# Differential attention on one core: attention by query blocks, with each head's last steps issued inside the next head

## What is computed

```python
def block(args):
    qb, bi = args
    ...
    bias = jnp.where(rel[None] >= 0, -slopes[:, None, None] * rel[None].astype(jnp.float32), -jnp.inf)
    s = jnp.einsum('bqhcd,bkhcd->bhcqk', qb, k).astype(jnp.float32) * scale
    p = jax.nn.softmax(s + bias[None, :, None], axis=-1)
    w = p[:, :, 0] - lam * p[:, :, 1]
    return jnp.einsum('bhqk,bkhe->bqhe', w.astype(v.dtype), v)
...
o = rmsnorm(o, subln_g, SUBLN_EPS) * (1.0 - lam_init)
return o.reshape(B, S, V_WIDTH) @ w_o
```

## Time and profile before

| | us |
|---|---|
| median of 3 runs | 1158.46 (1155.45 to 1159.59) |
| the profiled execution, device time | 1158.65 |
| its span, first to last instruction | 1156.8 |
| TensorE busy | 1109.6 (96%) |
| VectorE busy | 613.1 (53%) |
| ScalarE busy | 472.9 (41%) |
| GpSimd busy | 108.4 (9%) |

### The profile page before, as it was taken

The page is one execution under the profiler, slowest core; times in us unless marked ns, Lnnn a source line. Parts: engine busy times, 40 slices in busy tenths (PEclk is TensorE's granted clock), DMA queues, the critical chain, the costliest instruction groups (busy, mean ns, idle before and its releaser), DMA issues.

```text
span 1156.8 us, 13824 instructions
## 1 busy us (share of the span) xinstructions
PE 1109.6 (96%) x4854; PEld 883.9 (76%) x4854; DVE 613.1 (53%) x940; ACT 472.9 (41%) x731; POOL 108.4 (9%) x95
## 2 busy tenths in 40 slices
PE   8999999999999999999999899889999999999995
PEld 4676788888888888888866566668888888888884
DVE  4676965434434434446477877866433433433434
ACT  5475754313313313434246456654422322322342
POOL 0000021000000000021013322322000000000023
PEclk8999999999999999999999999999999999999998
DMA  5222232332322232233221111123223223223322
GB/s 206 73 73 73 73 110 92 99 102 91 97 103 91 92 107 91 92 108 107 76 74 37 54 37 54 37 73 100 101 92 109 92 91 106 94 91 101 98 73 73
DMA packets 30293, 102.42 MB, mean 89 GB/s; under 512 B 3248, under 2 KB 5552, under 8 KB 30128
## 3 DMA queue, kind: packets, MB, share of 16 engines
q1 hardware_dynamic: 29968, 100.74, 26.1%
q10 hardware_dynamic: 288, 1.18, 0.3%
HBM read 99.81 MB, written 2.10 MB: 88 GB/s over the span
## 4 chain that ended last, share of the span: by engine, by line
PE 83%; DVE 10%; ACT 4%; issue 2%; DMA 1%; SPq 0%; DVEq 0%; ACTq 0%
PE ps L1249 73%; PE ps L1380 4%; ACT prob L663 2%; PE ps L1443 1%; DVE prob L1140 1%; DVE w_lo L780 1%; DVE prob L1137 1%; PE ps L1417 1%; PE ps L1308 1%; DVE lru_v L874 1%; DVE inv_lam L1135 1%; ACT w_hi L430 1%; PE ps L1313 1%; DVE lru_v L907 1%; DMA w_raw<-weights 1%
## 5 line engine op out<-in xcount | busy, mean ns | idle before, releaser
L430 ACT ACTIVATE w_hi<-w_raw 128x1024 fp32r<-128x1024 f32 x184 | 193.6, 1052 | 240.9 <-PE ps L1249 205.3
L1249 PE MATMUL ps<-h_hi,w_hi 128*128 128x512 f32 x704 | 287.9, 409 | 2.9 <-DVE w_lo L780 2.9
L1249 PE MATMUL ps<-u_hi,w_hi 128*128 128x512 f32 x696 | 279.9, 402 | 4.2 <-DVE u_lo L918 1.9
L1249 PE MATMUL ps<-h_hi,w_lo 128*128 128x512 f32 x704 | 278.0, 395 | 0.0
L1249 PE MATMUL ps<-h_lo,w_hi 128*128 128x512 f32 x704 | 277.6, 394 | 0.0
L1249 PE MATMUL ps<-u_hi,w_lo 128*128 128x512 f32 x696 | 271.1, 390 | 0.0
L1249 PE MATMUL ps<-u_lo,w_hi 128*128 128x512 f32 x696 | 271.0, 389 | 0.0
L780 DVE TENSOR_TENSOR w_lo<-w_raw,w_hi 128x1024 fp32r<-128x1024 f32 x176 | 216.7, 1231 | 29.6 <-ACT w_hi L430 29.5
L1249 PEld LDWEIGHTS ps<-h_hi,w_hi 128*128 128x128 f32 x704 | 134.4, 191 | 36.8 <-DVE w_lo L780 4.6
L1249 PEld LDWEIGHTS ps<-u_hi,w_hi 128*128 128x128 f32 x696 | 130.7, 188 | 37.8 <-issue 5.9
L1249 PEld LDWEIGHTS ps<-h_lo,w_hi 128*128 128x128 f32 x704 | 134.5, 191 | 31.8 <-issue 4.7
(11 more groups left out here) (163 smaller groups left out, 885.1 us busy)
## 6 DMA issues: line engine op xcount, KB each, us to landing
w_raw<-weights SPq DMA_DIRECT2D x184, 512.0 KB, 3.3
x<-x_t SPq DMA_DIRECT2D x8, 256.0 KB, 7.3
y_t<-att SPq DMA_DIRECT2D x8, 256.0 KB, 2.3
gw<-gate_weights ACTq DMA_DIRECT2D x1, 1024.0 KB, 5.4
lam_in<-lam_vecs ACTq DMA_DIRECT2D x1, 128.0 KB, 2.4
vec<-vectors SPq DMA_DIRECT2D x1, 64.5 KB, 4.1
```

The costliest lines, as they stand in the source:

```text
L430: nc.scalar.activation(w_hi[:, t % RING, :], w_raw[:, t % RAWS, :], ACT.Copy).then_inc(whi_done, 1)
L1249: ins = nc.tensor.matmul(ps[:, bank, :], w[:, slot, ws], o[:, k, :], start=(k == 0 and n == 0), stop=(k == NCH - 1 and n == 2))
```

## The change

- The eight heads are written out; the hardware loops over pairs of heads are gone.
- `scores` takes float32 operands for all four j. The copies and subtractions that made `kq_hi` and `kq_lo` are gone, and `kq` has two buffers.
- `combined` no longer divides: it forms p0 + ratio * p1 with ratio = -lambda * total0 / total1, so a row stays larger by the factor total0. The norm that follows is indifferent to it; its epsilon is multiplied by total0 squared in `variance`. One pass over the row is left of two.
- `attend` is done by query block j, right after `transposed` of it: `prob_t` is the stationary operand, a slice of `value` the moving one, and the result has the query on the partition. GpSimd's `value_h` is gone. 10 float32 matmuls of 128 columns take the place of 4 of 128 to 512 columns.
- The norm's sums run along the free dimension: four 128-wide squares with sums on ScalarE (`squares`), all else on 128x4 numbers (`variance`, `sub_guess_of`, `sub_newton`, on VectorE and ScalarE), four 128-wide scalings (`scaled`), then `back` turns the head with four 128x128 transposes. `attended_hi` and `attended_lo` split it from bank 6 straight into `att_hi` and `att_lo`. `sub_sum` is gone.
- GpSimd has no work in the attention; VectorE makes `w_lo` of all tiles.
- Transposes 2 and 3, all four value products and the norm of head h are issued within head h+1, and the last head has a new interleaving with the output projection.

```diff
-            pool.wait_ge(bank_read, T_QK)
-            head_values(0, None, 0)
-            head_values(1, None, 1)
-            head_split_lo(0, None)
-            with pool.Fori(0, (HEADS - 2) // 2) as i:
-                own.enter(i, 4)
-                for k in range(2):
-                    head_values(2 + k, i, k)
-                    sub_newton(k, i)
-                    head_split_lo(1 + k, i)
-                own.leave((HEADS - 2) // 2)
-            head_split_lo(HEADS - 1, None)
-            sub_newton(HEADS - 2, None)
...
+            def squares(h):
+                act.wait_ge(att_mm, QB * (h + 1))
+                for j in range(QB):
+                    ins = nc.scalar.activation(o_square[:, rows(j)], ps[:, BANK_O, rows(j)], ACT.Square,
+                                               accum_out=o_stats[:, h % 2, 0, j:j + 1])
+                ins.then_inc(att_sq, 1)
+
+            def scaled(h):
+                act.wait_ge(sub_rstd, h + 1)
+                if h:
+                    act.wait_ge(back_mm, h)
+                for j in range(QB):
+                    ins = nc.scalar.activation(o_rows[:, rows(j)], ps[:, BANK_O, rows(j)], ACT.Copy,
+                                               scale=o_stats[:, h % 2, 4, j:j + 1])
+                ins.then_inc(o_scaled, 1)
+
+            def attended_hi(h):
+                act.wait_ge(back_mm, h + 1)
+                nc.scalar.activation(att_hi[:, h, :], ps[:, BANK_T, :], ACT.Copy,
+                                     scale=lam_s[:, 6:7]).then_inc(ohi_done, 1)
...
+            for h in range(HEADS):
+                last = h == HEADS - 1
+                if h:
+                    transposed(h - 1, 2)
+                split_hi(T_QK + 2 * h + 1 + RING if not last else T_QK + 2 * h + RING)
+                exps(h, 0)
+                if h:
+                    transposed(h - 1, 3)
+                exps(h, 1)
+                if h:
+                    squares(h - 1)
                 if last:
+                    split_hi(T_QK + 2 * h + 1 + RING)
+                    sub_guess_of(h - 1)
+                transposed(h, 0)
+                if last:
+                    exps(h, 2)
+                if h:
+                    if not last:
+                        sub_guess_of(h - 1)
+                    scaled(h - 1)
+                transposed(h, 1)
                 if not last:
+                    exps(h, 2)
+                if h < HEADS - 2:
+                    split_hi(T_QK + 2 * h + 2 + RING)
                 if last:
+                    exps(h, 3)
+                if h:
+                    attended_hi(h - 1)
                 if not last:
+                    exps(h, 3)
+            h = HEADS - 1
+            transposed(h, 2)
+            transposed(h, 3)
+            squares(h)
+            sub_guess_of(h)
+            scaled(h)
+            attended_hi(h)
...
+            def combined(h, j):
+
+
                 n = (QB - j) * P
                 s = j % 2
-                dve.wait_ge(exp_done, at(a + 1, i, 2 * QB))
-                own.step(nc.vector.reciprocal(inv[:, s, :], total[:, s, :]))
-                own.wait()
-                own.step(nc.vector.tensor_tensor(inv_lam[:, s:s + 1], inv[:, s, 1:2], neg_lam, ALU.mult))
-                own.wait()
-                own.step(nc.vector.tensor_scalar(prob[:, s, 1, 0:n], prob[:, s, 1, 0:n],
-                                                 inv_lam[:, s:s + 1], None, ALU.mult))
-                own.wait()
-                nc.vector.scalar_tensor_tensor(out=prob[:, s, 0, 0:n], in0=prob[:, s, 0, 0:n],
-                                               scalar=inv[:, s, 0:1], in1=prob[:, s, 1, 0:n],
+                dve.wait_ge(exp_done, QB * h + j + 1)
+                own.step(nc.vector.reciprocal(inv[:, s:s + 1], total[:, h % 2, j, 1:2]))
+                own.wait()
+                own.step(nc.vector.scalar_tensor_tensor(
+                    out=ratio[:, s:s + 1], in0=inv[:, s:s + 1], scalar=neg_lam,
+                    in1=total[:, h % 2, j, 0:1], op0=ALU.mult, op1=ALU.mult))
+                own.wait()
+                nc.vector.scalar_tensor_tensor(out=prob[:, s, 0, 0:n], in0=prob[:, s, 1, 0:n],
+                                               scalar=ratio[:, s:s + 1], in1=prob[:, s, 0, 0:n],
                                                op0=ALU.mult, op1=ALU.add).then_inc(prob_done, 1)
...
+            def variance(h):
+
+
+                first = total[:, h % 2, :, 0:1].rearrange("p q o -> p (q o)")
+                own.step(nc.vector.scalar_tensor_tensor(
+                    out=o_stats[:, h % 2, 3, :], in0=first, scalar=SUBLN_EPS, in1=first, op0=ALU.mult,
+                    op1=ALU.mult))
+                dve.wait_ge(att_sq, h + 1)
+                own.wait()
+                nc.vector.scalar_tensor_tensor(
+                    out=o_stats[:, h % 2, 1, :], in0=o_stats[:, h % 2, 0, :], scalar=1.0 / V_DIM,
+                    in1=o_stats[:, h % 2, 3, :], op0=ALU.mult, op1=ALU.add).then_inc(var_done, 1)
+
+            def attended_lo(h):
+                dve.wait_ge(ohi_done, O_ATT + h + 1)
+                nc.vector.scalar_tensor_tensor(out=att_lo[:, h, :], in0=ps[:, BANK_T, :],
+                                               scalar=sub_gain, in1=att_hi[:, h, :], op0=ALU.mult,
+                                               op1=ALU.subtract).then_inc(olo_done, 1)
...
+            for h in range(HEADS - 2):
+                query(h + 1)
+                split_lo(T_QK + 2 * h + 1 + RING)
+                biased(h, 3)
+                combined(h, 2)
+                key(h + 1)
+                if h:
+                    attended_lo(h - 1)
+                split_lo(T_QK + 2 * h + 2 + RING)
+                halved(h)
+                biased(h + 1, 0)
+                combined(h, 3)
+                biased(h + 1, 1)
+                combined(h + 1, 0)
+                combined(h + 1, 1)
+                variance(h)
+                biased(h + 1, 2)
+                sub_newton(h)
...
+                    pe.wait_ge(bank_read, T_QK + 2 * h + 2)
+                if a >= 2:
+                    pe.wait_ge(scores_read, 2 * (a - 1))
+                for c in range(2):
+                    rows = slice(c * HEAD_DIM, (c + 1) * HEAD_DIM)
+                    ins = nc.tensor.matmul(ps[:, BANK_SCORES + 2 * (j % 2) + c, 0:n],
+                                           kq[rows, h % 2, 1, qb * P:(qb + 1) * P],
+                                           kq[rows, h % 2, 0, 0:n], start=True, stop=True)
                 ins.then_inc(scores_mm, 1)
...
+            def attend(h, j):
+                a = QB * h + j
+                qb = QB - 1 - j
+                pe.wait_ge(trans_read, a + 1)
+                if h and j == 0:
+
+                    pe.wait_ge(o_scaled, h)
+                for kb in range(qb + 1):
+                    ins = nc.tensor.matmul(ps[:, BANK_O, qb * P:(qb + 1) * P],
+                                           prob_t[:, j % 2, kb * P:(kb + 1) * P],
+                                           value[:, kb, h * P:(h + 1) * P], start=(kb == 0),
+                                           stop=(kb == qb))
                 ins.then_inc(att_mm, 1)
 
+            def back(h):
+
+                pe.wait_ge(o_scaled, h + 1)
+                pe.wait_ge(trans_read, min(QB * (h + 1) + 2, QB * HEADS))
+                for qb in range(QB):
+                    qs = slice(qb * P, (qb + 1) * P)
+                    ins = nc.tensor.transpose(ps[:, BANK_T, qs], o_rows[:, qs], ident[:, :])
+                ins.then_inc(back_mm, 1)
...
+            for h in range(HEADS - 1):
+                kq_part(h + 1, 0)
+                scores(h, 0)
+                if h:
+                    transposes(h - 1, 2)
+                    attend(h - 1, 0)
+                scores(h, 1)
+                if h:
+                    attend(h - 1, 1)
+                kq_part(h + 1, 1)
+                scores(h, 2)
+                if h:
+                    transposes(h - 1, 3)
+                kq_part(h + 1, 2)
+                if h:
+                    attend(h - 1, 2)
+                    attend(h - 1, 3)
+                kq_part(h + 1, 3)
+                transposes(h, 0)
+                kq_part(h + 1, 4)
+                transposes(h, 1)
+                kq_part(h + 1, 5)
+                scores(h, 3)
+                kq_part(h + 1, 6)
+                if h:
+                    back(h - 1)
+                kq_part(h + 1, 7)
...
+            h = HEADS - 1
+            attend(h - 1, 0)
+            output_part(T_O, (0, 1))
+            transposes(h - 1, 2)
+            attend(h - 1, 1)
+            scores(h, 0)
+            transposes(h - 1, 3)
+            scores(h, 1)
+            output_part(T_O, (2, 3))
+            attend(h - 1, 2)
+            output_part(T_O, (4, 5))
+            attend(h - 1, 3)
+            output_part(T_O + 1, (0, 1))
+            scores(h, 2)
+            transposes(h, 0)
```

(58 more changed lines are left out.)

365 lines of the change are left out of this document (81 added, 284 removed).

## The result

| | us |
|---|---|
| before, median of 4 | 1156.95 (1155.19 to 1159.59) |
| changed kernel, median of 4 | 1129.99 (1128.45 to 1131.19) |
| ratio | 0.9764, 95% interval 0.9737 to 0.9792 |
| the profiled execution of the changed kernel | 1128.45, span 1126.7 |
| predicted | 1132.5, range 1129.0 to 1144.0 |

The kernel became 27 us faster where 26.0 were forecast. First the table of waits of TensorE in the changed kernel, from the last tiles of the shared key and value projection to behind the output projection; it answers to the earlier trace rows.

The account below looks back on a forecast made before the run. TensorE was taken to set the time while waiting for probabilities, as GpSimd blocks VectorE. Waits 20.1 and 5.4 plus clock 4.8, less 3.6 extra work and 0.7 new waits, gave 26.0 us: 1132.5 us, range 1129 to 1144.

Parts of the forecast that it names:

- The bound: Attention: TensorE sets the time but waits for prob; GpSimd blocks VectorE's third combined, an excess of 3.1 us.
- Waits, 20.1 + 5.4 us: TensorE in the attention: waits of transposes for prob go, 20.1 us; other waits go, 5.4; 0.4 for w_lo stays.
- Clock, 4.8 us: Heads 1 to 6: three falls of TensorE's clock behind the waits go, 1.59 us each, 4.8 us.
- TensorE's extra work, +0.45 per head: Scores +0.33, 64-row entry and exit +0.42, sub_sum -0.91, back +0.47, more pieces +0.1; taken as 3.6 us in 8 heads.
- The rival of 1150 us: Value product: weight loads of the float32 passes show, 0.11 each, 2.2 us per head, 17.6 in all; chance 0.07.
- What is late next: Head of 18.6 us: VectorE 14.2 and ScalarE 11.9 busy fit; all new waits charged 0.7 us.
- The margin of the norm's round trip: From value product to back: round trip some 5.5 us against 6.9 us of TensorE work between, margin 1.4 us.
- The sum: Whole kernel: 20.1 + 4.8 + 5.4 - 3.6 - 0.7 = 26.0 us gained, median 1132.5 us.
- New short waits: Attention cycle: small margins pass delays on, one us in each head, 1140.5 us; chance 0.15 together with VectorE staying slow.
- Dearer float32: Scores or value product: 64-row float32 pairs do not overlap (1143.5 us) or weight loads show (1150); chance 0.13.
- VectorE still slow with a small loss (1140.5): VectorE's queue: 3.1 us stay though GpSimd is idle, key late by at most 1 us per head; chance 0.15 with new waits.
- Slower by the norm: Norm's round trip makes TensorE wait in every head, 4.3 us per head at 5.7 excess, 1167 us; chance 0.04.

Follow-up runs that it names:

- e4: Kernel before, with GpSimd's w_lo of each attention head made by VectorE ahead of the fourth combined: 1143.4 us against 1157.51, ratio 0.9877.
- e5: Kernel before, with only the third transposition of every head issued one part (six matmuls) later: 1153.17 us, ratio 0.997.
- e8: Changed kernel with GpSimd kept busy by four scratch subtractions (6.4 us) in each of seven heads, at the old place: 1130.13 us, ratio 0.9778.
- e3: Changed kernel with six unused 512-wide ScalarE copies (4.0 us) ahead of the four scalings of each head's norm: 1150.02 us, ratio 0.9934.
- e10: Kernel before, third transposition one part later and GpSimd's w_lo on VectorE, but behind the fourth combined: 1147.05 us, ratio 0.9907.
- e6: Kernel before, with scores in one float32 product for all four blocks instead of three split products: 1159.22 us, ratio 1.0012.
- e2: Changed kernel with the 64-row scores of heads 0 to 6 issued in two excursions instead of four: 1125.74 us, ratio 0.9721.
- e1: Changed kernel with one w_lo per head (six tiles) given back to GpSimd: 1130.97 us, 0.35 more than the changed kernel.
- e9: Kernel before, with GpSimd's w_lo on VectorE ahead of the fourth combined and the third transposition one part later: 1141.62 us, ratio 0.9867.

## Why the prediction was right, point by point

**The bound.** Right that TensorE waits for probabilities and that VectorE is late because of GpSimd (e4: 2.44 back to 0.48 us). The same instruction has 0.48 us in the changed kernel too, under the 0.6 that was forecast:

```profile
629.40 0.48 DVE L1080 SCALAR_TENSOR_TENSOR prob<-prob,ratio 128x256 f32<-128x256 f32 x1
```

The excess was read too small, 3.1 us. One instruction ahead of the earlier trace rows, in the kernel before, one column takes 1.05 us for 0.16, so it is 4.0:

```profile
635.58 1.05 DVE L1135 TENSOR_TENSOR inv_lam<-inv,lam_s 128x1 f32<-128x1 f32 x1
```

Nor was GpSimd idle all through the quick ones of the earlier trace rows: its `w_lo` started at 748.44, inside the second, which had started first and was not held. Incomplete in the rest: I read the third transposition as the place where a head loses 2.9 us, and took the remainder for TensorE's own work. Moving just that step in the old kernel gave 0.15 us per head (e5). The claim that the new order or an idle GpSimd alone removes this wait holds for the changed kernel as a whole (e8: 2.12 us of `combined`, no wait in the loop). For an idle GpSimd in the old one it is not shown: e4 got rid of GpSimd's `w_lo` alone, and 1.0 us of wait stayed, but the Newton steps still held VectorE for 0.9 and 1.1 us there, more than the wait that was left.

**Waits, 20.1 + 5.4 us.** Right: 0.9 us of idle time is left of 23.6. I had said that the 0.4 for `w_lo` stays; it is 0.7.

**Clock, 4.8 us.** Right: no fall in the attention, and e4 and e5 had none either; a head with a fall has 22.86 us for 21.25, 1.6 as reckoned. The falls come with the long waits: e3, with 2.1 us of wait per head, has two. The one in the last head of e10 shows that several short waits in a row can do it too.

**TensorE's extra work, +0.45 per head.** Too much. A new head is 18.51 us where I had 18.7. Old heads without fall and wait take 18.2 to 18.3 (21.25 less 2.88 in front of the third transposition and 0.16 in front of the next scores; with a fall, 22.86 less 2.99 and 1.59), so the real difference is +0.2 to +0.3. The scores are +0.33 as reckoned (e6), the toll 0.38 for 0.42 (e2), and the rest is my surcharge of 0.1 for more pieces and rounding up. The float32 passes of 128 columns hide their loads of weights:

```profile
622.17 0.83 PE L1382 MATMUL ps<-value,prob_t 128*128 128x128 f32 x6
622.76 0.48 PE L1193 MATMUL ps<-u_hi,w_hi 128*128 128x512 f32 x1
623.08 0.39 PE L1193 MATMUL ps<-u_lo,w_hi 128*128 128x512 f32 x1
```

From the first of six passes to the second matmul behind them, less one 0.23, are 0.68 us: 0.11 each, with six loads, and a quarter of the 0.43 of a 512-column pass is 0.11. (The next matmul is recorded as starting inside the last pass, so the distance to it alone, 0.59 us, is too short; the 0.10 of a transpose in the prediction is 0.11 for the same reason.) The rule of the Trainium skill (TensorE: Matmul & The Clock Gate, The mechanism) that a load overlaps matmuls in flight only across row groups does not hold for these full-array passes. The same section lets a load run ahead if it goes to a background weight buffer, which would fit; no run here tells. The rival of 1150 us, where each load shows, is out. In both kernels a toll does appear where 64-row and 128-row work alternate.

**What is late next.** Nothing in the loop, as forecast. VectorE has 75.47 / 6 = 12.6 us of work in a head where I had 14.2; 0.7 of that is the `w_lo`, 1.2 us where I took 1.9, and 0.9 the slow `inv_lam` that I had missed. ScalarE has 67.16 / 6 = 11.2 for 11.9. The margin of the norm's round trip was put at 1.4 and is 1.7 (e3), but not by my sum: a 128-wide square follows the last one after 0.25 to 0.27 us where I took the 0.40 of an exponential from the earlier trace rows, and the copy of the second transposition, which stands behind the scalings and is what `back` waits for in e3, was not in it.

```profile
623.04 0.28 ACT L630 ACTIVATE work<-ps 128x128 f32<-128x128 f32 x1
623.21 0.20 ACT L630 ACTIVATION_READ_ACCUMULATOR work<-ps 128x1 f32 x1
623.31 0.27 ACT L630 ACTIVATE work<-ps 128x128 f32<-128x128 f32 x1
```

**The sum.** The stretch took 194.1 us where 221.1 less 26.0, 195.1, was forecast. The 1.0 us between is the extra work, 8 x 0.2 = 1.6 too much, less what the waits and the last head came to in detail, which I did not split further.

**The rivals.** New short waits: two, 0.9 us in all, none in the loop. Dearer float32: pairs out by e6, loads by the passes of 0.11. VectorE still slow with a small loss (1140.5): the case was made in e8, and the loss is nil; the 1 us per head came from stacking the delay on a queue whose idle time (1.9 us before `key`) I had counted too low. Slower by the norm: not so, and by e3 it was 1.7 us away.

## What to carry to other kernels

When the busiest engine waits in each turn of a loop, find out whether one slow step or the length of the whole turn holds it: move the step that is waited for by one place. If the turn stays as long, the wait only walks on; then letting the turn run over into the next is worth a try. Before an order is judged, look at which instructions of VectorE and GpSimd run side by side; one GpSimd pass of 2.4 us there held a 0.5 us instruction for 2.4 us, and the same pass in VectorE's idle time cost nothing (e1). And once TensorE has no idle time left, count its switches between 64-row and 128-row work: at 0.38 us each they were worth another 5 us.

## What was unexpected

The clock of TensorE falls behind some long waits, but not in each execution. Near 40 and 105 us of the recurrent layer, behind waits of 2.4 and 2.0 us that are as long in every run, the profiled execution of the kernel before has two falls, that of the changed kernel none, its repetition one, e1 and e2 two. The same instructions then end up to 3.1 us apart, which is the size of the spread of a kernel's runs here (1128.45 to 1131.19). In the attention, waits of 1.0 us (e4, e9) and 1.6 us (e5) were followed by no fall in any head before the last, waits of 2.9 us by one in every second head, and of 2.1 to 2.4 us (e3) by two in seven. What decides within these was not tried.

A running GpSimd instruction holds up even the smallest ones of VectorE: one column (1.04 us instead of 0.16) or four (0.97). It leaves those alone that read one of their two operands from PSUM. The Trainium skill's rule on two SBUF inputs (SBUF — State Buffer, Who interferes with whom) says as much, and e8 shows both sides of it within 6 us.
